# Three landing buffers for a stream of weight slabs, and two kinds of slabs interleaved, in a float32 decoder step

## The reference, cut to what matters

```python
q = (xt @ w_q)                       # 8 heads, two halves each
s = einsum('thpc,hpkc->thpk', q, sub_keys)      # 128 keys for each half
...                                  # top 16 by 16 candidates -> 16 experts a head, softmax gates g
u = take(u_tab, idx);  act = gelu(einsum('ted,td->te', u, x))
w = g * act
v = take(v_tab, idx);  out = einsum('te,ted->td', w, v)
```

## Time and profile before

| what | value |
|---|---|
| median of 3 runs | 2171.46 us (2166.41 to 2171.79) |
| the profiled execution, its own time | 2170.59 us |
| its span, first to last instruction | 2168.8 us |
| PE busy | 2079.0 us, 96% |
| DVE busy | 1639.0 us, 76% |
| ACT busy | 964.7 us, 44% |
| mean granted TensorE clock | 0.989 of full |
| slab transfers | 592 of 512 KB |

### The profile page before, as it was taken

One profiled execution on the slowest core, in us unless ns is written; L12 is line 12 of the kernel. 1 busy time (PEld: TensorE's weight loads), 2 busy tenths in 40 slices (PEclk: granted clock), 3 DMA queues, 4 the chain that ended last, 5 costly groups with the idle time before them and its releaser, 6 DMA issues.

```text
span 2168.8 us, 40396 instructions
## 1 busy us (share of the span) xinstructions
PE 2079.0 (96%) x16458; PEld 1895.1 (87%) x16458; DVE 1639.0 (76%) x3068; ACT 964.7 (44%) x1642; POOL 334.1 (15%) x245
## 2 busy tenths in 40 slices
PE   8999999999999999979998999999999999999988
PEld 7899989999899987767897999999998899877766
DVE  7887995556877778757699779965658876888666
ACT  5654453434433433334655544534344433333344
POOL 0013000000000075332110050000000000656310
PEclk9999999999999999999999999999999999999999
DMA  5343544444544557776431434544445544567763
GB/s 174 108 155 124 169 156 154 152 157 159 175 162 142 159 180 236 245 253 203 136 92 61 141 127 153 168 147 151 155 151 176 167 149 144 166 230 257 246 210 117
DMA packets 112935, 358.34 MB, mean 165 GB/s; under 512 B 17264, under 2 KB 27760, under 8 KB 112496
## 3 DMA queue, kind: packets, MB, share of 16 engines
q1 hardware_dynamic: 99888, 319.99, 45.7%
q0 software_dynamic: 12288, 33.60, 4.8%
q10 hardware_dynamic: 576, 2.18, 0.2%
HBM read 349.09 MB, written 6.63 MB: 164 GB/s over the span
## 4 chain that ended last, share of the span: by engine, by line
PE 52%; DVE 23%; DMA 16%; ACT 6%; issue 2%; POOL 0%; SPq 0%; DVEq 0%; ACTq 0%
DMA land<-stream_dram 16%; PE ps L878 11%; PE ps L879 10%; PE ps L880 10%; DVE w_lo L1470 8%; ACT w_hi L583 5%; PE ps L909 5%; PE ps L911 5%; PE ps L910 5%; PE ps L956 4%; DVE work L1356 1%; DVE work L1592 1%; DVE work L1597 1%; DVE hidden L1671 1%; DVE hidden L1356 1%
## 5 line engine op out<-in xcount | busy, mean ns | idle before, releaser
L1470 DVE TENSOR_TENSOR w_lo<-land,w_hi 128x1024 fp32r<-128x1024 f32 x562 | 686.6, 1222 | 362.5 <-ACT w_hi L583 360.0
L583 ACT CAST w_hi<-land 128x1024 fp32r<-128x1024 f32 x592 | 621.2, 1049 | 620.7 <-DMA land<-stream_dram 575.8
L878 PE MATMUL ps<-act_hi,w_hi 128*128 128x288 f32 x2688 | 810.6, 302 | 19.9 <-DVE act_lo L1196 6.2
L879 PE MATMUL ps<-act_hi,w_lo 128*128 128x288 f32 x2688 | 795.5, 296 | 0.0
L880 PE MATMUL ps<-act_lo,w_hi 128*128 128x288 f32 x2688 | 792.7, 295 | 0.0
L878 PEld LDWEIGHTS ps<-act_hi,w_hi 128*128 128x128 f32 x2688 | 506.2, 188 | 28.0 <-issue 16.8
L880 PEld LDWEIGHTS ps<-act_lo,w_hi 128*128 128x128 f32 x2688 | 508.4, 189 | 0.0
L879 PEld LDWEIGHTS ps<-act_hi,w_lo 128*128 128x128 f32 x2688 | 507.5, 189 | 0.8
L909 PE MATMUL ps<-w_hi,g_hi 128*128 128x512 f32 x1024 | 411.5, 402 | 29.1 <-DVE g_lo L1745 29.0
L910 PE MATMUL ps<-w_lo,g_hi 128*128 128x512 f32 x1024 | 402.6, 393 | 0.0
L911 PE MATMUL ps<-w_hi,g_lo 128*128 128x512 f32 x1024 | 402.3, 393 | 0.0
(11 more groups left out here) (214 smaller groups left out, 1351.6 us busy)
## 6 DMA issues: line engine op xcount, KB each, us to landing
land<-stream_dram SPq DMA_DIRECT2D x592, 512.0 KB
act_d<-smp_stage SPq DMA_DIRECT2D x64, 64.0 KB, 3.3
hidden<-stream_dram,smp_idx POOLq DMA_INDIRECT x128, 4.9
x<-x_dram SPq DMA_DIRECT2D x4, 288.0 KB, 5.3
y_t_dram<-hidden SPq DMA_DIRECT2D x8, 144.0 KB, 1.9
work<-keys_dram SPq DMA_DIRECT2D x1, 1024.0 KB, 7.6
smp_act<-act_d,smp_idx POOLq DMA_INDIRECT x64
work<-keys_dram ACTq DMA_DIRECT2D x1, 1024.0 KB, 6.2
```

The costliest lines, as they stand in the source:

```text
L583: nc.scalar.copy(w_hi[:, m, :], land[:, n % LANDS, :]).then_inc(w_hi_ready, 1)
L878: nc.tensor.matmul(out, w_hi[:, slot, wsl], hi, start=start, stop=False)
L879: nc.tensor.matmul(out, w_lo[:, slot, wsl], hi, start=False, stop=False)
L1470: V.tensor_tensor(w_lo[:, k, :], land[:, n % LANDS, :], w_hi[:, k, :].bitcast(F32), ALU.subtract).then_inc(lo_by_dve, 1)
```

## The change

Three things change. `LANDS` goes from 2 to 3: the tile `land` grows by 4 KB a partition, and SP waits for slab n - 3 where it waited for n - 2. To pay for part of it, `STAGE` goes from 16 to 8 (2 KB down to 1 KB a partition, two groups of four in place of four), and the store of a group stands 7 positions after its last slab (`STORE_LAG`), not 8. In `layer_slabs` the 32 U slabs 96 to 127 move from behind block 0's 32 V slabs to between them: two V slabs and two U slabs in turn, sixteen times, over the same positions 136 to 199. Everything computed from the order (the visits, the positions of block 1's gate chunks) follows; the data's layout in HBM stays as it is.

```diff
-LANDS = 2
+LANDS = 3
...
     for e in range(*BLOCKS[0], 2):
         visit(e, (1, 0))
-    slabs += [("U", stream_u(e), e) for e in range(HELD, P)]
+        slabs += [("U", stream_u(k), k) for k in range(HELD + e, HELD + e + 2)]
...
-STAGE, GROUP = 16, 4
+STAGE, GROUP = 8, 4
 RINGS = STAGE // GROUP
-STORE_LAG = 8
+STORE_LAG = 7
```

## The result

The changed kernel takes 2099.73 us (median of 4 runs, 2098.25 to 2101.20) against 2170.28 us; the ratio is 0.9678, with a 95% interval of 0.9661 to 0.9694. The forecast was 2119 us with a range of 2101 to 2150. The profiled execution took 2101.2 us (span 2099.4).

What follows compares the result with a forecast made beforehand. PE was taken as the bound except where the two-buffer landing trip (6.68 us, a slab every 3.34) starves it. Terms 35 + 5.7 + 2.5 + 7 + 2 - 1.3 = 51 us from 2170.6 gave 2119 us, range 2101 to 2150.

Steps and rivals of the forecast that it cites:

- 245 to 284: Slab stream of both layers: PE takes over from the two-buffer trip as the bound; 35 us gain, bounds 19 and 38.
- 226 to 244: Positions where DVE is nearly full: half of the 11.4 us lost returns, 5.7 us; bounds 0 and 11.4.
- 200 to 225: Late one-hots with a lighter DVE: 2.5 of 3.3 us lost return; bounds 0 and 3.3.
- 40 to 75: The picks, where DVE is the bound: 3.5 us a layer, 7 us gained; bounds 0 and 11.3.
- interleaving: Mixed U and V slabs: nothing to win as PE has no idle time; 1.3 us lost to added changes.
- the burst: ACT's 2 MB of keys and conv state in layer 0, delaying a landing to 9.73 us; 1.5 us left for it.
- The condition itself: Positions 245 to 284: landings should mostly stay below 5.95 us, at a load of 284 GB/s, before three buffers bind.
- The echo behind it: U slabs behind the picks: 1 us a layer, 2 us gained; bounds 0 and 5.8.
- Everything comes back: Rival: all lost time in all rows is recovered, 70 us, giving 2101; nearly all recovered, below 2108, 0.10.
- Landings grow with the load: Rival: mean landing 7 us keeps 28 us lost, 2144; longer landings or a full DVE, 2132 to 2150, 0.20.
- The change doesn't do it: Rival: w_hi slots hold ACT's casts, so the third buffer only stands full; 2172 us, chance 0.03.
- slower: Rival: the ring of 8 stops ACT because stores land late; 2215 us with 1.5 us each, chance 0.04.

Runs made afterwards that it cites:

- e11_gathers_dense: Changed kernel with the sample additions and their gathers packed into positions 244 to 284 in place of 226 to 284; 2105.57 us, 2167.83 for the kernel before.
- e8_more_dve_after: Changed kernel with one more 128-column DVE operation at each of positions 226 to 244 of each layer; 2104.03 us.
- e10_twice_the_dve: Changed kernel with two more 128-column DVE operations at each of positions 226 to 244 of each layer; 2115.56 us.
- e3_light_adds_before: Kernel before with DVE's sample additions cut to 64 of their 1024 columns; 2159.04 us, 2165.82 for the kernel before on that chip.
- e9_more_dve_before: Kernel before with one more 128-column DVE operation at each of positions 226 to 244 of each layer; 2171.58 us, 2168.39 without.
- e7_ring_alone: Kernel before with only the ring of 8 sample tiles and stores one position earlier, two landing buffers; 2167.16 us, 2167.83 for the kernel before.
- e1_order_back: Changed kernel with the U slabs back behind block 0's V slabs, keeping three buffers and the ring of 8; 2099.34 us.

## Why the forecast was wrong

What each term was to bring and what the windows of the two kernels show:

| positions | forecast | layer 0 | layer 1 | together |
|---|---|---|---|---|
| 245 to 284 | 35 | 134.2 - 112.1 = 22.1 | 126.8 - 108.8 = 18.0 | 40.1 |
| 226 to 244 | 5.7 | 67.4 - 61.6 = 5.8 | 67.8 - 61.5 = 6.3 | 12.1 |
| 200 to 225 | 2.5 | 85.8 - 82.7 = 3.1 | 84.0 - 82.7 = 1.3 | 4.4 |
| 40 to 75 | 7 | 125.8 - 120.6 = 5.2 | 125.2 - 120.5 = 4.7 | 9.9 |
| 76 to 135 | 2 | 1.0 | 2.2 | 3.2 |
| interleaving | -1.3 | -0.6 | -0.6 | -1.2 |
| elsewhere | 0 | | | 0.9 |
| sum | 51 | | | 69.4 |

**The step that failed** is the one for positions 226 to 244: "The idle time goes, the load stays, and two engines at 98% that wait for each other don't run without gaps. I take half, 5.7 us". What came back is 12.1 us, nearly all. The load was read rightly: DVE has 60.71 us of work, PE needs 61.0 (e11_gathers_dense; the forecast had 60.9), and the window became 61.6, the larger of the two plus 1%. e8_more_dve_after and e10_twice_the_dve confirm that DVE is nearly full there. What was wrong is the idea that two full engines cost each other half of what the buffers had cost: they cost each other 0.6 us a layer at most. How far DVE's work and a buffer's trip cost each other with two buffers, e3_light_adds_before and e9_more_dve_before leave open; with three, the longer engine sets the window to 1%.

**Positions 245 to 284** were mis-sized by 5.1 us. The pace of PE came out of idle time and clock as 2.77 us a slab; it is 2.72 (51.7 / 19). The shown idle time and clock are short of the loss; that a matmul's modelled end covers part of a gap would explain it and is not shown. So 43 us were lost there and not 38, and 3.3 us stayed, all in the burst, where I had left 3. The same measure was short at 226 to 244 (11.4 us counted, 135.2 - 2 x 61.0 = 13.2 lost) and at 200 to 225 (3.3 counted, 4.4 came back). In all three places the gain lies above the upper bound that I had given: some 8 of the missing 18.5 us are this second failed step, the loss taken as idle time plus clock. The condition itself was right: the load came out at 300 and 265 GB/s, 281 over the two windows of layer 0 where 284 was forecast, and a landing, 5.5 us at most in the median, stayed below the 5.95 us allowed. The landings before were read too narrowly: "4.3 to 5.1 us now" is two of them, and the chain of 894 to 962 us has others from 3.95 to 5.89 us.

**The picks (40 to 75)** gave 9.9 us and not 7. The step "DVE's chain can shorten by at most its 5.2 us" held as a number: 5.2 and 4.7 us. I had taken two thirds of that bound without a row that spoke for the discount. The path is right only in part: in the changed kernel's waits of 184 to 305 us DVE's idle time for casts is still 1.7 us, so 3.5 of the 5.2 us are casts that come earlier, and the rest is not traced; PE's wait for ACT's evacuation is gone from the list, and its wait for the picks is 1.6:

```profile
DVE w_lo L1470 <- ACT w_hi L583: 1.7, 5, 0.7
...
PE ps L1053 <- issue: 1.6, 1, 1.6
```

The echo behind it and positions 200 to 225 missed in the same way, by 1.2 and 1.9 us. The discounts in four rows and the mis-sized loss make up 17.5 of the 18.5 us.

**What held.** The cause (the trip of a buffer over the number of buffers), the neutral interleaving within 0.1 us, the ring of 8 at no cost (e7_ring_alone), the position of PE as the next bound, and the burst as what stays.

**The rivals.** *Everything comes back* was the right one; it stood at 0.10 with a time of 2101. The argument against it, DVE's 60.04 us, was an argument for a window of 61 us and not against it. Its time was too high, as its sum used the losses that were measured short. *Landings grow with the load* is real, and did not reach PE: the median landing is 4.4 to 5.5 us with three buffers and 4.0 to 4.5 with two, where the rival needed 7. It takes the dense gathers to lose 1.4 us in 21 slabs, and the burst to lose more. The Trainium skill puts HBM's latency at 2 us at high load (DMA: Bandwidth & Descriptors, Latency and other measured facts). The traces show about 1 us at most of the 1.8 that the estimate took from it, and the estimated 14 us kept lost did not come. *The change doesn't do it* and *slower* are excluded by e1_order_back and e7_ring_alone.

**The range** ended at full recovery by my own undersized measure of the loss, 2101. With the pace of a clean window, 2.7 us a slab, the loss at 245 to 284 would have been 134 + 126 - 80 x 2.7 = 44 us and the lower end about 2095.

## What to carry to other kernels

When a chain repeats transfer, step, step, and then the next transfer waits for the last step, the pace is the trip over the number of buffers. Compare it with the pace of the engine that ought to be the bound, and if one more buffer puts it below, with landings as long as the new load makes them, forecast the full recovery: here the larger of the engines' busy times plus 1%. A discount needs a row of its own, and "both are nearly full" is not one. Take the loss from the clean pace of an unstarved window, not from the idle time shown. And when the stream runs ahead, look for the one large transfer that still cuts through it: moving it by 21 slabs gave another 3 to 4 us by the windows (5.2 between the medians).

## What was not expected of the hardware

An operation of 128 columns on DVE is shown with 285 ns, but it moves its neighbour by less, since the shown times of neighbours overlap in part. In e8_more_dve_after:

```profile
831.44 0.29 DVE L1755 TENSOR_TENSOR work<-ident,iota 128x128 f32<-128x128 f32 x1
831.64 1.28 DVE L1671 SCALAR_TENSOR_TENSOR hidden<-hidden,smp_act 128x1024 f32<-128x1024 f32 x1
```

The next operation starts 0.20 us after it. Two in a row, with a wait between them, take 0.53 us in e10_twice_the_dve (832.20 to 832.73). So what an added small operation costs a full engine is less than its shown duration.

A slab issued into the 2 MB burst, two transfers on ACT's queue beside the slabs of SP's queue and POOL's gathers, took 10.24 us to land, and 9.73 us before: a third buffer did not shorten it. More buffers hide such a landing in part.
